# Score products without a narrow remainder, and a 16-row remainder moved to partitions 32 to 47, in a streaming attention and mLSTM step

## What is computed

```python
aq, ak, av, mq, mk, mv, ig, lf, og = project(rms_norm(x, norm1_g), w_in, ...)
# differential attention, 4 heads of 2 x 128; a stream sees 256 cached keys and its 16 new ones
s = einsum('bqhcd,bkhcd->bchqk', aq, concat([cache_k, ak])) * 128 ** -0.5 + bias
w = softmax(s[:, 0]) - lam * softmax(s[:, 1])
o = einsum('bhqk,bkhd->bqhd', w, concat([cache_v, av]))
# mLSTM memory, 4 heads: D is the decay of every earlier position, the state carries the past
A = exp(D - mt) * einsum('bthd,bshd->bhts', mq, mk)
num = einsum('bhts,bshe->bthe', A, mv) + iw * einsum('bhed,bthd->bthe', C, mq)
C_new = dec * C + einsum('bhs,bshe,bshd->bhed', sw, mv, mk)
h = rms_norm(num / den) * sigmoid(og)
x = x + concat([att, h]) @ w_out
y = x + square(relu(rms_norm(x) @ w_up)) @ w_down
```

## Time and profile before

| | |
|---|---|
| median of 3 runs | 1760.07 us (1758.96 to 1760.13) |
| profiled execution | 1760.2 us |
| its span on the core | 1758.4 us, 27423 instructions |
| PE busy | 1751.1 us (100%) |
| weight loads on PE | 1589.7 us (90%) |
| DVE busy | 893.8 us (51%) |
| ACT busy | 675.4 us (38%) |
| POOL busy | 178.0 us (10%) |
| granted TensorE clock | full in all 40 slices |
| DMA | 261.55 MB, mean 149 GB/s |
| chain that ended last | PE 98%, DVE 1% |

### The profile page before, as it was taken

One profiled execution on the slowest core, in us unless ns is written; L12 is line 12 of the kernel. 1 busy time (PEld: TensorE's weight loads), 2 busy tenths in 40 slices (PEclk: granted clock), 3 DMA queues, 4 the chain that ended last, 5 costly groups with the idle time before them and its releaser, 6 DMA issues.

```text
span 1758.4 us, 27423 instructions
## 1 busy us (share of the span) xinstructions
PE 1751.1 (100%) x9430; PEld 1589.7 (90%) x9430; DVE 893.8 (51%) x1702; ACT 675.4 (38%) x1272; POOL 178.0 (10%) x235
## 2 busy tenths in 40 slices
PE   9999999999999999999999999999999999999999
PEld 8999999999987789999888999888999888999887
DVE  5634776666677545554344454344444334545333
ACT  5323754444454444333333333333333333333332
POOL 3301010001121210110000110000111000111000
PEclk9999999999999999999999999999999999999999
DMA  7675479988778554444334443334444334444442
GB/s 185 191 175 149 123 169 221 210 194 208 194 242 275 147 136 117 125 126 123 129 124 127 121 130 120 132 120 131 119 125 126 125 126 127 124 121 130 139 149 96
DMA packets 380178, 261.55 MB, mean 149 GB/s; under 512 B 91676, under 2 KB 327388, under 8 KB 380108
## 3 DMA queue, kind: packets, MB, share of 16 engines
q1 hardware_dynamic: 353190, 222.09, 44.7%
q0 software_dynamic: 11856, 34.68, 7.3%
q10 hardware_dynamic: 15062, 3.86, 1.1%
HBM read 244.90 MB, written 21.46 MB: 151 GB/s over the span
## 4 chain that ended last, share of the span: by engine, by line
PE 98%; DVE 1%; ACT 0%; issue 0%; POOL 0%; ACTq 0%; POOLq 0%; DVEq 0%
PE acc L518 18%; PE acc L519 18%; PE acc L520 18%; PE bank L605 8%; PE bank L606 8%; PE bank L604 8%; PE bank L1869 3%; PE ssb L604 2%; PE ssb L605 2%; PE ssb L606 2%; PE ssb L1869 1%; PE bank L564 1%; PE bank L565 1%; PE bank L563 1%; PE acc L563 1%; PE acc L565 1%
## 5 line engine op out<-in xcount | busy, mean ns | idle before, releaser
L498 DVE TENSOR_TENSOR w_lo<-raw,w_hi 128x512 fp32r<-128x512 f32 x768 | 556.6, 733 | 780.2 <-ACT w_hi L489 779.5
L489 ACT ACTIVATE w_hi<-raw 128x512 fp32r<-128x512 f32 x768 | 482.6, 630 | 842.9 <-PE acc L520 409.7
L519 PE MATMUL acc<-x2g_lo,w_hi 128*128 128x384 f32 x1024 | 348.0, 340 | 0.0
L518 PE MATMUL acc<-x2g_hi,w_hi 128*128 128x384 f32 x1024 | 345.8, 338 | 0.0
L520 PE MATMUL acc<-x2g_hi,w_lo 128*128 128x384 f32 x1024 | 344.6, 337 | 0.0
L518 PE MATMUL acc<-a_hi,w_hi 128*128 128x400 f32 (+1 forms) x768 | 268.1, 349 | 0.2 <-DVE w_lo L498 0.2
L519 PE MATMUL acc<-a_lo,w_hi 128*128 128x400 f32 (+1 forms) x768 | 262.9, 342 | 0.0
L520 PE MATMUL acc<-a_hi,w_lo 128*128 128x400 f32 (+1 forms) x768 | 262.3, 341 | 0.0
L605 PE MATMUL bank<-w_lo,a_hi 128*128 128x512 f32 x640 | 253.0, 395 | 0.0
L606 PE MATMUL bank<-w_hi,a_lo 128*128 128x512 f32 x640 | 252.6, 395 | 0.0
L604 PE MATMUL bank<-w_hi,a_hi 128*128 128x512 f32 x640 | 252.0, 394 | 0.0
(11 more groups left out here) (336 smaller groups left out, 1506.2 us busy)
## 6 DMA issues: line engine op xcount, KB each, us to landing
raw<-in_w_up SPq DMA_DIRECT2D x128, 512.0 KB, 4.0
raw<-in_w_down SPq DMA_DIRECT2D x128, 512.0 KB, 3.7
raw<-in_w_in SPq DMA_DIRECT2D x94, 512.0 KB, 4.7
raw<-in_w_out SPq DMA_DIRECT2D x32, 512.0 KB, 4.2
vc<-in_cache_v POOLq DMA_DIRECT2D x32, 256.0 KB, 6.4
kc<-in_cache_k SPq DMA_DIRECT2D x128, 64.0 KB, 3.2
state_blocks<-in_state_C POOLq DMA_DIRECT2D x16, 256.0 KB, 4.4
C_blk<-state_blocks SPq DMA_DIRECT2D x4, 1024.0 KB, 8.7
```

The lines of the kernel that those rows point to most:

```text
L489: e.activation(w_hi[:, q], raw[:, slot, 4 * (q % 2):4 * (q % 2) + 4, :], ACT.Copy).then_inc(hi_ready, 1)
L498: e.tensor_tensor(w_lo[:, q], raw[:, slot, 4 * (q % 2):4 * (q % 2) + 4, :], w_hi[:, q].bitcast(F32), ALU.subtract).then_inc(lo_ready, 1)
L518: e.matmul(out, w_hi[:, q, kk], hi[:, k, at], start=k == 0, stop=False, skip_group_check=True)
L519: e.matmul(out, w_hi[:, q, kk], lo[:, k, at], start=False, stop=False, skip_group_check=True)
```

## The change

Five edits:

1. kT grows to 272 keys. DVE copies the stream's 16 new keys into it ahead of the last key transpose, and each score product takes all 272 columns.
2. ko moves to memory that n_sq and n_y use during the key norm, so its first transpose waits for all eight norms (n_done 8) in place of the first keys' landing, and SyncE's load of tile 41 waits for ko's stores.
3. The prompt's last 16 memory rows lie on partitions 32 to 47. Their transposes take 48 columns, the 32 before them included.
4. In num the banks of both prompt groups are claimed at once. Each group's last product is 32 rows deep, one on partitions 0 to 31, the other on 32 to 63, and they are issued behind each other. The last product of cp is 32 rows deep too.
5. DVE's step of og goes to slot 8, after that slot's w_lo; ACT's stays at 7.

```diff
+TAIL_AT = 32
+TAIL_ROWS = slice(TAIL_AT, TAIL_AT + TAIL)
+LATE_GROUP, TAIL_GROUP = slice(0, 32), slice(TAIL_AT, TAIL_AT + 32)
...
-           ("take0", 4), ("take1", 5), ("take2", 5), ("take3", 6), ("num", 6), ("hsum", 6), ("cp", 7), ("og", 7),
+           ("take0", 4), ("take1", 5), ("take2", 5), ("take3", 6), ("num", 6), ("hsum", 6), ("cp", 7), ("og", 7), ("og_late", 8),
...
+        with ExitStack() as s:
+            ko = sb("ko", [P, 2, 13, 32], scope=s)
...
-            kT = sb("kT", [P, 8, PAST], scope=s)
+            kT = sb("kT", [P, 8, KEYS], scope=s)
...
                 if t == STATE_LOADS[0]:
-                    e.wait_ge(S("n_done"), 8)
+                    for x in range(2):
+                        e.wait_ge(S(f"ko_out{x}"), 16 * 4 * 4)
...
                     elif what == "ko":
-                        if n == 0:
-                            e.wait_ge(S("kc_in0"), 64)
-                        elif n >= 2:
+                        if n >= 2:
                             e.wait_ge(S(f"ko_out{n % 2}"), 16 * 4 * (n // 2))
-                        e.wait_ge(S("n_done"), 5 + n // 2)
+                        e.wait_ge(S("n_done"), 8)
...
+                        if i == 3:
+                            q0 = NPR + b * TD
+                            e.wait_ge(S("n_done"), 8)
+                            e.tensor_copy(kT[:, :, PAST:KEYS], zt[:, 8:16, q0:q0 + TD])
...
-                            mm(out[:, 0:PAST], q, kT[:, hc], True, True)
-                            last = mm(out[:, PAST:KEYS], q, zt[:, 8 + hc, q0:q0 + TD], True, True)
+                            last = mm(out[:, 0:KEYS], q, kT[:, hc], True, True)
...
-                    elif what == "og":
+                    elif what == "og_late":
                         e.wait_ge(S("og_step"), 3 * h + 3)
...
+            def memory_row_blocks(tile):
+
+                return [*row_blocks(tile)[0:3], (3 * P, tile[:, STARTS[3] - TAIL_AT:STARTS[3] + TAIL])]
...
-                b = fill(e, ("num", 1, h))
-                mm(b[:, 0:DVX], expo[:, P:2 * P], v_rows[:, 1], True, False)
-                filled(mm(b[:, 0:DVX], expo[:, late:late + P], v_rows[:, 2], False, True), ("num", 1, h))
-                b = fill(e, ("num", 2, h))
-                mm(b[:, 0:DVX], expo[:, 2 * P:3 * P], v_rows[:, 1], True, False)
-                mm(b[:, 0:DVX], expo[:, late + P:late + 2 * P], v_rows[:, 2], False, False)
-                filled(mm(b[:, 0:DVX], expo[:, tail:tail + P], v_rows[:, 3], False, True), ("num", 2, h))
+                first, second = fill(e, ("num", 1, h)), fill(e, ("num", 2, h))
+                mm(first[:, 0:DVX], expo[:, P:2 * P], v_rows[:, 1], True, False)
+                mm(second[:, 0:DVX], expo[:, 2 * P:3 * P], v_rows[:, 1], True, False)
+                mm(second[:, 0:DVX], expo[:, late + P:late + 2 * P], v_rows[:, 2], False, False)
+                filled(mm(first[:, 0:DVX], expo[LATE_GROUP, late:late + P], v_rows[LATE_GROUP, 2], False, True),
+                       ("num", 1, h))
+                filled(mm(second[:, 0:DVX], expo[TAIL_GROUP, tail:tail + P], v_rows[TAIL_GROUP, 3], False, True),
+                       ("num", 2, h))
...
                 for r in range(1, 4):
-                    mm(b[:, 0:DVX], k_swp[:, r - 1], v_rows[:, r], r == 1, r == 3)
+                    rows = slice(0, P) if r < 3 else TAIL_GROUP
+                    mm(b[:, 0:DVX], k_swp[rows, r - 1], v_rows[rows, r], r == 1, r == 3)
```

More of the change, by code:

```diff
@@ L1098, in head_work @@
                         e.wait_ge(S("expo_pre"), h + 1)
[L1099 to L1103, removed]
+                        for lo, hi_, r, rows in ((0, P, 0, slice(0, P)), (P, EXPO_LATE, 1, slice(0, P)),
+                                              (EXPO_LATE + P - META, EXPO_TAIL, 2, slice(0, P)),
+                                              (EXPO_TAIL + P - TAIL, EXPO_TAIL + P, 3, TAIL_ROWS)):
+                            last = e.activation(expo[rows, lo:hi_], expo[rows, lo:hi_], ACT.Exp,
+                                                bias=cols[rows, 0, r, h:h + 1])
                         last.then_inc(S("expo_exp"), 1)
@@ L1346, in gate @@
                     e.tensor_copy(cols16[:, 4:7], psum16[:, 4:7])
-                    e.tensor_copy(cols16[0:TAIL, 3], psum16[0:TAIL, 3])
-                    taken(e.tensor_copy(cols16[0:TAIL, 7], psum16[0:TAIL, 7]), "gcols")
+                    e.tensor_copy(cols16[TAIL_ROWS, 3], psum16[TAIL_ROWS, 3])
+                    taken(e.tensor_copy(cols16[TAIL_ROWS, 7], psum16[TAIL_ROWS, 7]), "gcols")
             def gate_work():
@@ L1529, in att_work @@
                             done(e, ("n", 7, 1))
-                        e.transpose(kT[:].rearrange("p c (x r) -> p x c r", r=32)[:, 2 * i:2 * i + 2],
+                        if i == 3:
+                            q0 = NPR + b * TD
+                            e.wait_ge(S("n_done"), 8)
+                            e.tensor_copy(kT[:, :, PAST:KEYS], zt[:, 8:16, q0:q0 + TD])
+                        e.transpose(kT[:, :, 0:PAST].rearrange("p c (x r) -> p x c r", r=32)[:, 2 * i:2 * i + 2],
                                     kc[:, i].rearrange("p (x c d) -> p x c d", x=2, d=32)).then_inc(S("blocks_turned"), 1)
@@ L1617, in weigh @@
                 tt(expo[:, 0:128], expo[:, 0:128], sx[:, 0:128], ALU.mult)
-                late, tail = expo[:, EXPO_LATE + P - META:EXPO_TAIL], expo[0:TAIL, EXPO_TAIL + P - TAIL:]
+                late, tail = expo[:, EXPO_LATE + P - META:EXPO_TAIL], expo[TAIL_ROWS, EXPO_TAIL + P - TAIL:]
                 tt(late, late, sx[:, 128:272], ALU.mult)
-                taken(tt(tail, tail, sx[0:TAIL, 272:288], ALU.mult), ("sx", h))
+                taken(tt(tail, tail, sx[TAIL_ROWS, 272:288], ALU.mult), ("sx", h))
                 sy = take(e, ("sy", h))
@@ L1699, in enter @@
                 e.memset(v_rows[:, 0:3, DV:DVX], 1.0)
-                e.memset(v_rows[0:TAIL, 3, DV:DVX], 1.0)
+                e.memset(v_rows[TAIL_ROWS, 3, DV:DVX], 1.0)
                 e.memset(q_iw[:], 0.0)
@@ L1940, in gate_work @@
                             for r in range(4):
-                                last = e.transpose(b[0:ROWS[r], 4 * (4 * a + r):4 * (4 * a + r) + NH],
-                                                   row[0:NH, STARTS[r]:STARTS[r] + ROWS[r]], ident[0:NH, 0:NH])
+                                n, from_ = (ROWS[r], STARTS[r]) if r < 3 else (TAIL_AT + TAIL, STARTS[r] - TAIL_AT)
+                                last = e.transpose(b[0:n, 4 * (4 * a + r):4 * (4 * a + r) + NH],
+                                                   row[0:NH, from_:from_ + n], ident[0:NH, 0:NH])
                         filled(last, "gcols")
@@ L1969, in turn_av, with turn_rows @@
                 turn_rows(("av", n), m1[:, n])
-            def turn_rows(key, tile):
+            def turn_rows(key, tile, blocks=row_blocks):
                 b = fill(e, key)
-                for at, src in row_blocks(tile):
+                for at, src in blocks(tile):
                     last = e.transpose(b[0:src.shape[1], at:at + P], src, ident[:])
@@ L2104, in head_work @@
                         e.wait_ge(S(f"mv_in{h % 2}"), 16 * (h // 2 + 1))
-                        turn_rows(("kn", h), m1[:, 4 + h])
+                        turn_rows(("kn", h), m1[:, 4 + h], memory_row_blocks)
                         for x in range(2):
-                            turn_rows((f"vn{x}", h), mvo[:, h % 2, x])
+                            turn_rows((f"vn{x}", h), mvo[:, h % 2, x], memory_row_blocks)
                     elif what == "scores":
```

9 lines of the change are left out of this document (4 added, 5 removed).

## The result

| | before | after |
|---|---|---|
| median of 15 runs | 1759.38 us (1758.86 to 1760.33) | 1762.50 us (1761.59 to 1764.21) |
| ratio after to before | | 1.0018, 95% interval 1.0011 to 1.0025 |
| profiled execution, its span | 1758.4 us | 1760.5 us |
| PE busy, matmuls | 1751.1 us, 9430 | 1751.7 us, 9302 |
| granted TensorE clock | full in all slices | full in all slices |

The change costs 3.1 us, 0.18%. That is just within the 0.2% that I had set as the limit of what can be told from nothing, but the interval of the ratio lies wholly above 1: with 15 runs of each it is a real, small loss. The number was forecast as 1761.3 (1759.3 to 1763.3), so it lies inside the range and 1.2 us above its middle. The forecast of a change within 0.2% holds, but the sum behind it was too small by half: two terms were missing.

A forecast was written before the change was run, and what follows sets the result against it. TensorE (PE) was taken as the bound, busy 1751.1 of 1758.4 us. Terms -0.8 + 0.2 - 0.1 + 1.1 - 0.4 + 0.4 + 0.8 = +1.2 us gave a median forecast of 1761.3 us, range 1759.3 to 1763.3.

The forecast's parts named there:

- Scores: Score products: 64 narrow ones removed and 64 widened save 0.10 us in each of 8 streams, -0.8 us.
- The copy: DVE's copy of the new keys ahead of stream 0's last key transpose delays PE by +0.2 us; later streams hide it.
- The pair: Numerators' last two 32-row products side by side on two row groups: -0.1 us over heads 0, 2 and 3.
- State update: Its last product, 32 rows deep and alone, costs +0.37 us a head, +1.1 us for heads 0, 2, 3.
- Gate step (a): DVE's gate step one slot later, head 1: PE's wait for the last input tile's emptying shrinks, -0.4 us.
- (b): DVE's gate step one slot later, head 2: the output sum ends later and PE waits for its bank, +0.4 us.
- Gate step (c): DVE's gate step one slot later, heads 0 and 3: no similar consumer due soon after, so no cost.
- Both banks claimed at once: Numerators: PE waits for bank 1 ahead of the first product, +0.8 us in head 3, nothing in heads 0 to 2.
- rival 3: The numerators' last two products run one after the other: 1763.3 us, 8%.
- against 1: Rival: changes of the array's division cost nothing and busy time is time, 1755.8 us, 3%.
- against 4: Rival: neither new PE wait (head 2's output sum, head 3's bank 1) shows, 1760.1 us, 14%.
- Rival 2: ACT's 0.9 us delay before its next w_hi reaches PE at all four heads, 1764.5 us, 5%.

The follow-up runs named there:

- run 2: The changed kernel with the state update's last product 128 rows deep again, remainder still on partitions 32 to 47; 1760.93 us.
- run 7: The kernel before with only the state update's last product 32 rows deep, on partitions 0 to 31; 1760.82 us.
- run 1: The changed kernel with DVE's gate step (og) back at slot 7; 1761.30 us.
- run 9: The kernel before with only DVE's gate step moved to slot 8 in all four heads; 1760.31 us.
- run 3: The changed kernel with the numerators as before: bank 1 claimed after bank 0's products, all 128 rows deep, one after the other; 1761.49 us.
- run 4: The kernel before with only the last 16 memory rows moved to partitions 32 to 47, with 48-column transposes; 1760.09 us.
- run 5: The kernel before with the 16 rows on partitions 32 to 47, but small operations and last score product covering partitions 0 to 47; 1759.93 us.
- run 6: The kernel before with only the 16 rows moved, to partitions 64 to 79, with 80-column transposes; 1760.46 us.
- run 10: The changed kernel with DVE's weigh step at slot 2 instead of 3; 1761.21 us.

## Why the prediction was right, and by less than it seems

- **Scores**, -0.8: right. The block is 1.35 (1.32 to 1.36 was announced), 0.09 less a stream from the second on.
- **The copy**, +0.2: mis-sized. It takes 0.21 us on DVE as I said, but PE starts stream 0's products only 0.1 later: 1.57 to 1.59 us behind the weight product in front of that wait in the eight traces with the copy, 1.43 to 1.51 in the six without it. I charged the copy's whole record; DVE starts the transpose 0.13 behind the copy's start, before the copy has ended, and PE follows the transpose's end by 0.10 us in all traces.

```profile
264.02 0.21 DVE L1536 COPY kT<-zt 128x128 f32<-128x128 f32 x1
264.15 0.71 DVE L1537 STREAM_TRANSPOSE kT<-kc 128x512 f32<-128x512 f32 x1
```

- **The pair**, -0.1: right, 0.04 a head. Weighing the 1.7 us that follow from the Trainium skill (TensorE: Matmul & The Clock Gate, Part 3) against the rows of a block with the same ways in and out was the step that kept this from being forecast as a gain. The trace shows six full passes and two waves of pairs, the two products of a wave 0.007 us apart, so they do run together. Two passes fewer save 0.43; in front of the waves stand 0.31 and 0.32 us instead of 0.22, and from the last wave to L523 it is 0.59 where it was 0.39: 0.39 are spent again.
- **State update**, +0.37 a head: right, 0.39, with head 1's swallowed as said (runs 2 and 7).
- **Gate step (a)**, -0.4 and **(b)**, +0.4: right (runs 1 and 9: -0.41, +0.45).
- **Gate step (c)**, "Heads 0 and 3 have nothing of this kind: no output sum or accumulator is due soon after": this step failed. I looked only for consumers of the kind found in head 2. Head 3 has another: h_rows empties a bank, and the transpose of n_new is the next to fill it. It cost 0.73 us. Bank 1's claim had been followed this way, from the bank to who frees it; here I did not do it (run 9: +0.71 with nothing else changed).
- **Both banks claimed at once**, +0.8: right, 0.80 together with the pair (run 3: 0.78 less).
- **The place of the remainder**: the prediction priced the 48-column transposes at nothing, which was right, and said no word on ACT's and DVE's operations "with the same shapes", so that they stand in the sum at nothing without a reason. This was the second failed step: 0.71 us. The shapes and the durations were the same, the start partition was not, and the cost lies between the records (runs 4 to 6). The wait that it lengthens, for weigh's bank, had no slack.

Sum: -0.72 + 0.71 + 1.07 - 0.37 + 0.45 + 0.80 + 0.73 = +2.67 against +1.2. The misses were 0.71 and 0.73 up, and 0.1 down at the copy. The medians say 3.1; the 0.4 between trace and medians is within what they can tell, and no run here divides it.

That the number lies inside the range is in part luck. It was built on 1760.07, the median of three runs of the kernel before; that of 15 is 1759.38. From there the same sum gives 1760.6, and the range ends at 1762.6, which 1762.50 only just meets. And the range's upper end was there for rival 3, the pair one after the other, which did not happen; two costs that I had not named filled its place.

The rivals: none came. The state update costs what was forecast (against 1), the pair runs side by side (against 3), both new waits show (against 4), and no wait for w_lo follows a root step (against 2). Rival 2 (ACT's delay reaches PE at every head) came nearest, in the wrong place: not through w_hi but through a bank, at one head more.

## What to carry to other kernels

When a step moves later, list every resource that the steps behind it give back, PSUM banks included, and find the next user of each; a search for the kind of wait that one already knows finds just those. When rows move to other partitions, compare the starts of each operation with its neighbours' on that engine: the cost stands between the rows, in none of them. And an edit of several parts that sums to little is worth taking apart: here two parts gain 0.7 and 0.4 us, four lose 3.8, and keeping the two with one more slot of slack gives the fastest kernel.

## What was unexpected of the hardware

- DVE and ACT operations that start at partition 32 or 64 between ones that start at 0 do not overlap with them, 0.1 us on either side; 48 rows from partition 0 take less time in the row of operations than 16 rows from partition 32 (0.89 against 1.13 us for four, runs 4 to 6).
- A pair of 32-row products on two row groups saves 0.04 us against two full products in their place, and a lone one costs 0.39 us over a full one. In front of the first pass of another division stand some 0.1 us more (0.31 instead of 0.22 before the pair, before the lone product and before the strips of the numerators; 0.27 instead of 0.18 before k_sw's strips in run 10), and where 32-row or full products follow, the second pass pays as much again (0.32 instead of 0.22).
